# Moving three buffers of a Trainium2 kernel to other SBUF addresses modulo 512

## The reference

```python
def memory_cross_attention(h, m, wq, wkv, wo):
    q = (h @ wq).reshape(B, S, XA_HEADS, XA_HEAD_DIM)
    kv = m @ wkv
    ...
    return o @ wo

def conv_ffn(h, w_up, conv_w, conv_b, w_down):
    z = h @ w_up
    u = z[..., :D_FF]
    g = dwconv3_centred(z[..., D_FF:], conv_w) + conv_b
    return (jax.nn.gelu(g, approximate=False) * u) @ w_down
```

## The kernel before

| buffer | address before | residue before | address after | residue after |
|---|---|---|---|---|
| H | 1152 | 128 | 1152 | 128 |
| XH | 17536 | 128 | 17536 | 128 |
| XL | 33920 | 128 | 34208 | 416 |
| w_raw, w_lo | 50304 | 128 | 50848 | 160 |
| w_hi | 70784 | 128 | 71328 | 160 |
| R | 91264 | 128 | 91808 | 160 |
| ACC | 95424 | 192 | 95904 | 160 |
| cst (ident, ones, causal) | 101632 | 256 | 102112 | 224 |
| HID, most of the arena | 103744 | 320 | 104352 | 416 |

## Time and profile before

### The profile page before, as it was taken

The page is one execution under the profiler, slowest core; times in us unless marked ns, Lnnn a source line. Parts: engine busy times, 40 slices in busy tenths (PEclk is TensorE's granted clock), DMA queues, the critical chain, the costliest instruction groups (busy, mean ns, idle before and its releaser), DMA issues.

```text
span 2469.0 us, 25636 instructions
## 1 busy us (share of the span) xinstructions
PE 2375.9 (96%) x10910; PEld 1924.1 (78%) x10910; DVE 999.7 (40%) x1222; ACT 863.7 (35%) x1044; POOL 983.7 (40%) x389
## 2 busy tenths in 40 slices
PE   8989999999999999999999999988998999999997
PEld 6748878888887887888887668867877888888885
DVE  4243034442143213444236231567368333666601
ACT  4245344233322433422344462351351243322221
POOL 4506524544444642444435324330240153456641
PEclk9999999999999999999999999999999999999998
DMA  7204313332332431333333213320220033333331
GB/s 185 94 17 143 114 43 95 102 94 94 94 96 92 147 101 52 94 101 95 105 104 111 68 43 101 111 69 18 60 77 18 26 94 129 99 97 94 98 95 63
DMA packets 148561, 218.23 MB, mean 88 GB/s; under 512 B 18640, under 2 KB 75216, under 8 KB 148192
## 3 DMA queue, kind: packets, MB, share of 16 engines
q1 hardware_dynamic: 147328, 212.38, 28.7%
q10 hardware_dynamic: 1120, 4.23, 0.5%
HBM read 212.34 MB, written 4.23 MB: 88 GB/s over the span
## 4 chain that ended last, share of the span: by engine, by line
PE 92%; DVE 5%; ACT 1%; issue 1%; DMA 0%; POOL 0%; SPq 0%; ACTq 0%; DVEq 0%
PE ps L928 76%; PE ps L1069 2%; PE ps L1072 2%; PE ps L1290 1%; PE ps L1085 1%; PE ps L1108 1%; DVE MT L1857 1%; PE ps L1279 1%; PE ps L1178 1%; PE ps L1191 1%; PE ps L1015 1%; PE ps L1231 1%; DVE MM L1861 0%; PE ps L951 0%; PE ps L1307 0%
## 5 line engine op out<-in xcount | busy, mean ns | idle before, releaser
L485 POOL TENSOR_TENSOR w_lo<-w_raw,w_hi 128x1024 fp32r<-128x1024 f32 x379 | 972.1, 2575 | 1444.2 <-ACT w_hi L522 1443.8
L928 PE MATMUL ps<-XH,w_hi 128*128 128x512 f32 x1792 | 703.2, 392 | 13.1 <-DVE XL L1418 12.2
L522 ACT ACTIVATE w_hi<-w_raw 128x1024 fp32r<-128x1024 f32 x379 | 395.3, 1055 | 892.6 <-DMA w_raw<-ffn_w_up 124.4
L928 PE MATMUL ps<-XH,w_lo 128*128 128x512 f32 x1792 | 698.4, 390 | 0.0
L928 PE MATMUL ps<-XL,w_hi 128*128 128x512 f32 x1792 | 698.1, 390 | 0.0
L928 PE MATMUL ps<-HID,w_hi 128*128 128x512 f32 x1760 | 554.7, 396 | 4.0 <-DVE TY L1640 2.4
L928 PEld LDWEIGHTS ps<-XH,w_hi 128*128 128x128 f32 x1792 | 337.1, 188 | 86.0 <-issue 14.6
L928 PEld LDWEIGHTS ps<-HID,w_hi 128*128 128x128 f32 x1760 | 330.2, 188 | 86.9 <-issue 3.4
L928 PEld LDWEIGHTS ps<-XL,w_hi 128*128 128x128 f32 x1792 | 337.2, 188 | 72.1 <-issue 2.4
L928 PEld LDWEIGHTS ps<-XH,w_lo 128*128 128x128 f32 x1792 | 337.0, 188 | 70.3
L928 PE MATMUL ps<-HID,w_lo 128*128 128x512 f32 x880 | 347.6, 395 | 0.0
(11 more groups left out here) (318 smaller groups left out, 2319.7 us busy)
## 6 DMA issues: line engine op xcount, KB each, us to landing
w_raw<-w_in SPq DMA_DIRECT2D x72, 512.0 KB, 3.7
w_raw<-ffn_w_up SPq DMA_DIRECT2D x128, 256.0 KB, 2.9
w_raw<-w_up SPq DMA_DIRECT2D x88, 256.0 KB, 3.1
w_raw<-xa_wkv SPq DMA_DIRECT2D x32, 512.0 KB, 3.7
w_raw<-ffn_w_down SPq DMA_DIRECT2D x32, 512.0 KB, 3.6
w_raw<-w_in_c SPq DMA_DIRECT2D x24, 512.0 KB, 3.7
w_raw<-w_down SPq DMA_DIRECT2D x22, 512.0 KB, 3.6
w_raw<-w_in_ab SPq DMA_DIRECT2D x16, 512.0 KB, 4.1
```

The source lines that it names most:

```text
L485: nc.gpsimd.tensor_tensor(w_lo[:, s, :, :], w_raw[:, s, :, :], w_hi[:, s, :, :].bitcast(F32), ALU.subtract).then_inc(lo_done, 1)
L522: nc.scalar.activation(w_hi[:, s, :, :], w_raw[:, s, :, :], ACT.Copy).then_inc(hi_done, 1)
L928: mm = nc.tensor.matmul(ps[:, bank + m, :], a, b, start=start and j == 0 and n == 0, stop=stop and j == 1 and n == 2)
```

## The change

The small tiles RC and LNC are moved between XH and XL and padded with an unused tile `shift`; a second unused tile, `shift2`, stands between XL and the rings; the arena's start is chosen from w_hi's address. RC and LNC have 16 bytes each but take 32 each, so the first padding adds 288 bytes and the second 256. No instruction is added, removed or moved: on every engine the instructions of before and after stand in the same order with the same operands' names and shapes. The differences of residue between the two operands of a matmul are these:

| pair | before | after |
|---|---|---|
| XH minus rings | 0 | -32 (480) |
| XL minus rings | 0 | 256 |
| HID, MH, ML minus rings | 192 | 256 |
| pairs within the arena | unchanged | unchanged |
| cst minus arena | -64 | -192 |

```diff
         H = sb("H", [P, KT, T])
         XH = sb("XH", [P, KT, T], F32R)
+        RC = sb("RC", [P, NCH])
+        LNC = sb("LNC", [P, NCH])
+        shift = sb("shift", [P, 64 - 2 * NCH])
         XL = sb("XL", [P, KT, T], F32R)
+        shift2 = sb("shift2", [P, 64])
         w_raw = sb("w_raw", [P, RING, 2, UC])
         w_lo = nc.alloc_sbuf_tensor_at("w_lo", [P, RING, 2, UC], F32R, offset=nc.sbuf_base - RING * 2 * UC * 4)
+        w_hi_at = nc.sbuf_base
         w_hi = sb("w_hi", [P, RING, 2, UC], F32R)
         R = sb("R", [P, T])
         LNT = sb("LNT", [P, T])
-        RC = sb("RC", [P, NCH])
-        LNC = sb("LNC", [P, NCH])
         ACC = sb("ACC", [P, T])
...
-        a0 = (nc.sbuf_base + 63) // 64 * 64
-        arena = sb("arena", [P, (BIG_SLOTS * T * 4 + TAIL + 64) // 4])
+        a0 = nc.sbuf_base + (w_hi_at + 256 - nc.sbuf_base) % 512
+        arena = sb("arena", [P, (BIG_SLOTS * T * 4 + TAIL) // 4])
```

## The result

The changed kernel takes 2483.5 us (median of 4 runs, 2482.46 to 2484.28) against 2466.84 us for the kernel before; the ratio is 1.007, 95% interval 1.0056 to 1.0084. It is slower by 0.7%, and the forecast was 2482.7 us. The size is right. The profile shows that it is not made of the terms of my sum, so that the agreement is luck.

The account below looks back on a forecast made before the run. The prediction took PE's matmul start-to-start step as the bound. XL +11.9 and +0.6, HID 0, MH and ML 0, XH +4.2 summed to +16.7 us on the 2466.0 us median: 2482.7 us, range 2425 to 2503.

Parts of the forecast that it names:

- The bound: Whole kernel: PE busy 96% of the span, so the distance between matmul starts sets the time.
- priced every wait at nothing: Loads, ACT, POOL and DVE beside the matmuls: still covered, no wait added, priced at 0.
- Between two equal neighbours 64 bytes away I take 233.3: 1800 x 6.6 ns = +11.9 us: XL moving over the rings, 0 to 256: takes the 233.3 ns of 192 and 320; bounds -20.2 and +23.8 us.
- By the same reading they stay at 233.3: 0: HID moving over the rings, 192 to 256, 2640 matmuls: no change; bounds -47.0 and +17.4 us.
- The same 0 for MH and ML: MH and ML at 192 to 256, L1072 and L1069: no change; bounds -3.4 and +1.3 us for each.
- A straight line from 0 to the 233.3 of 192 rises ... 1.1 ns: 3792 x 1.1 = +4.2 us: XH moving or loaded, 0 to -32: small rise in proportion to distance; bounds 0 and +25.0 us.
- my 16.7: Summed change, all from X: XL moving +11.9, XL loaded +0.6, XH +4.2 us.
- rival B: 256 acts like 0: HID falls to 226.7 ns, XL stays, XH half way up; 2458.5 us, chance 0.18.
- A: 256 is free of the collision: XL, HID, MH, ML drop to 215.5 ns; 2395.1 us, half form 2432.6; chance 0.27.
- D: 256 is the worst place, 192 and 320 its flanks, XH pays in full: +70.0 us, 2536.0 us; chance 0.07.
- Rival C: Addresses modulo 512 do nothing, region or tile distance sets the step: all steps stay, 2466.0 us; chance 0.12.
- The 215.5 ns that served as the lower bound: Step without any excess, from plain float32 matmuls of 256 columns, taken as equal in cycles to float32r of 512.

Follow-up runs that it names:

- the probe: Matmul blocks without the computation: at 4 bytes, 64 differences in 4-byte steps, 226.7 to some 240 ns; at 320, differences in steps of 32, 229.2 ns.
- The sweep: Computation left out, blocks of 48 float32r matmuls at differences 0 to 480 in steps of 32: 226.7 ns at 0 and 256, 233.5 at 32.

## Why the prediction came out right, and where its steps were wrong

The total was right by luck: three terms of the sum were wrong, and their errors cancelled.

**The bound** was right. TensorE's step sets the time, no instruction moved, and the change lies in the stretches of the float32r matmuls: +32.3 - 18.3 - 0.4 of 13.5 us of span, -0.1 for all else. I had also priced every wait at nothing. One was not: at the wait for w_lo about 2.7 us came back, as the result shows.

**"Between two equal neighbours 64 bytes away I take 233.3: 1800 x 6.6 ns = +11.9 us"** failed. Alone, XL at 256 measured 0 (ratio 1.000). The neighbours did not bound what lies between them, since the pattern repeats after 256 bytes and 256 is another 0. The 7 us that XL's steps did lose, 1800 x 4.0 ns, come with XH's shift, as the kernel with XH alone moved shows at XL difference 0.

**"By the same reading they stay at 233.3: 0"** for HID failed for the same reason: -18.3 us in the changed kernel, and 19 to 22 us of device time in the two kernels with the arena alone moved, 17 of them in the stretches of HID. The same 0 for MH and ML was nearly right because it holds two errors: -1.2 us where they are loaded, +0.8 where they move.

**"A straight line from 0 to the 233.3 of 192 rises ... 1.1 ns: 3792 x 1.1 = +4.2 us"** failed most. XH's steps rose by 7.6 ns, 27 us over the 3600 in which it moves; with XL's steps the shift of 32 bytes costs 33 us of span when it is made alone. Even my upper bound of 25.0 us was short. The cost is not a slope: it is all there at 32 bytes, and at 4 bytes the probe reads 237.2.

The errors cancel: the stretches of X came out 15.6 us above my 16.7, those of HID 18.3 below my 0, which leaves a miss of 3 us in the profiled spans and none in the medians. The mechanism of rival B with XH at a full step is what happened: -18 and +32 give about the +13.5 us of span. I had priced B at 2458.5 us, since I put XH half way up a slope that does not exist, and B too had the 256-column steps of MH and ML fall, where they rose. The sweep puts the others out. For A the step at 256 had to be near 216, for D near 240, and it was 226.8. Rival C (addresses do nothing) falls with the steps that moved with nothing but addresses changed. It is also where the Trainium skill's page "SBUF — State Buffer", section "SBUF: two separate sides", with its second independent read port for the weight load led.

The 215.5 ns that served as the lower bound was read from plain float32, where two records are one matmul. No float32r step of 512 columns reached it in any block.

**Still open** is the mechanism. That it is a collision of TensorE's two reads was argued from the difference being what counts; shown is that the excess depends on the difference, not on the region, is not below 13 ns in any block of 384 or 512 columns, and does not follow the size of the load. Why float32r has these 13 ns even at the best place, why matmuls of 256 columns prefer 128 or 192 to 0, and why the layout of the moving tiles enters at some differences, no run here tells. In the kernel before, ring moving and MH or ML loaded at 320 took 233.3 ns, and the probe at 320 took 229.2.

## What to carry to other kernels

Where a stream of float32r matmuls sets the time, read the distance between starts for each pair of buffers, and compare the pairs: 227 against 233 ns in one kernel is 3% of the slower one's time. For matmuls of 512 columns put moving and stationary buffers at the same residue modulo 256, and compute it from the address that the allocator gives, since here two tiles of 16 bytes that took 32 each turned a gain of 19 us (ratio 0.9928) into a loss of 17. For other sizes measure first: with 256 columns the same residue was the slower place, by 1 to 2 ns. Do not interpolate a cost over addresses; a sweep of 64 blocks takes one run of half a millisecond.

## What the runs showed of the hardware that was not expected

The step of float32r matmuls of 512 columns at full clock varied from 226.7 to some 240 ns with the difference of the operands' start addresses, in jumps of up to 13 ns between differences 4 bytes apart. At multiples of 32 bytes the pattern repeated after 256 bytes, and at the differences 0, 32 and 256 it was the same for four places of the stationary operand. A tile at a good difference still lost 4 ns when the tiles that moved before and after it lay at a bad one. With 256 columns the order was another: 119.9 ns at 0 and 256, 117.8 at 192. Loading a quarter of the columns left the step at 231.9 ns, longer than the 226.7 with all of them. Plain float32, with two passes a matmul and two cycles a column in each, showed none of this at three differences: 429.2 ns a pass.
